# Borders by token block, five weight slots and turned-back first chunks in a four-layer transformer kernel

## The reference

```python
for i in range(2):                       # first block
    y = mla_mixer(...) if i == 0 else dilated_mixer(...)   # on rms_norm(h, g[0])
    h = h + rms_norm(y, g[1])
    h = h + rms_norm(swiglu(rms_norm(h, g[2]), w_in, w_out), g[3])
    h = h + (p[i] @ ple_w_proj[i]) * sigmoid(h @ ple_w_gate[i])
for l in range(2):                       # second block
    mix = hybrid_mixer(x, w_in[l], ...)  # retention, block attention, convolution; then @ w_out
    x = layer_norm(ALPHA * x + mix, ...)
    f = (gelu(causal_dwconv(x @ w_up_a)) * (x @ w_up_b)) @ w_down
    x = layer_norm(ALPHA * x + f, ...)
```

## Time and profile before

| | us |
|---|---|
| median of 3 runs | 1621.08 (1620.62 to 1624.9) |
| the profiled execution | 1619.89 |
| its span in the trace | 1618.1 |
| PE busy | 1494.7 (92%) |
| POOL busy | 1060.0 (66%) |
| DVE busy | 840.3 (52%) |
| ACT busy | 756.2 (47%) |

### The profile page before, as it was taken

One profiled execution on the slowest core, in us unless ns is written; L12 is line 12 of the kernel. 1 busy time (PEld: TensorE's weight loads), 2 busy tenths in 40 slices (PEclk: granted clock), 3 DMA queues, 4 the chain that ended last, 5 costly groups with the idle time before them and its releaser, 6 DMA issues.

```text
span 1618.1 us, 26225 instructions
## 1 busy us (share of the span) xinstructions
PE 1494.7 (92%) x10190; PEld 1372.1 (85%) x10190; DVE 840.3 (52%) x1269; ACT 756.2 (47%) x856; POOL 1060.0 (66%) x255
## 2 busy tenths in 40 slices
PE   6897999998999999989999999779999797799996
PEld 5786999878999999789987789679998697599985
DVE  5546888024222322388841254567860458568833
ACT  6774554344544444555543445235543344255531
POOL 4254788865665555568887586358888575378883
PEclk9997999999999999989999999879999899799999
DMA  5383555545555555345555555335565555245551
GB/s 208 98 293 123 182 181 182 182 156 180 174 184 162 167 171 172 130 144 181 181 182 182 183 189 182 104 105 182 181 208 182 168 172 175 78 148 183 182 214 53
DMA packets 63346, 271.15 MB, mean 168 GB/s; under 512 B 5978, under 2 KB 28688, under 8 KB 36273
## 3 DMA queue, kind: packets, MB, share of 16 engines
q1 hardware_dynamic: 38300, 242.62, 44.3%
q10 hardware_dynamic: 24981, 27.61, 5.1%
HBM read 269.08 MB, written 8.21 MB: 171 GB/s over the span
## 4 chain that ended last, share of the span: by engine, by line
PE 83%; DVE 11%; ACT 4%; issue 1%; POOL 1%; DMA 0%; ACTq 0%; SPq 0%; DVEq 0%
PE psum L423 81%; DVE rstd L1337 2%; DVE newton L1331 1%; PE psum L740 1%; PE psum L530 1%; ACT w_hi L917 1%; ACT xt_hi L932 1%; DVE psum L1480 1%; DVE cv L1692 1%; DVE psum L1470 1%; POOL w_lo L403 1%; DVE h L1484 1%; DVE cv L1688 0%; DVE var L1716 0%; DVE xt_lo L1410 0%
## 5 line engine op out<-in xcount | busy, mean ns | idle before, releaser
L403 POOL TENSOR_TENSOR w_lo<-raw,w_hi 128x2048 fp32r<-128x2048 f32 (+3 forms) x251 | 1059.8, 4228 | 535.5 <-ACT w_hi L917 535.2
L917 ACT ACTIVATE w_hi<-raw 128x2048 fp32r<-128x2048 f32 (+3 forms) x251 | 450.2, 1794 | 515.9 <-PE psum L423 497.0
L423 PE MATMUL psum<-xt_hi,w_hi 128*128 128x256 f32 x1984 | 569.6, 287 | 7.1 <-DVE xt_lo L1410 5.8
L423 PE MATMUL psum<-xt_hi,w_lo 128*128 128x256 f32 x1984 | 565.9, 285 | 0.0
L423 PE MATMUL psum<-xt_lo,w_hi 128*128 128x256 f32 x1984 | 565.9, 285 | 0.0
L423 PEld LDWEIGHTS psum<-xt_hi,w_hi 128*128 128x128 f32 x1984 | 385.7, 194 | 14.8 <-issue 14.7
L423 PEld LDWEIGHTS psum<-xt_lo,w_hi 128*128 128x128 f32 x1984 | 385.7, 194 | 0.1
L423 PEld LDWEIGHTS psum<-xt_hi,w_lo 128*128 128x128 f32 x1984 | 385.3, 194 | 0.0
L423 PE MATMUL psum<-w_hi,xt_hi 128*128 128x384 f32 (+3 forms) x408 | 143.3, 364 | 15.7 <-DVE xt_lo L1414 9.5
L1443 DVE TENSOR_TENSOR conv<-conv,gate 128x256 f32<-128x256 f32 x44 | 144.8, 3292 | 1.5
L423 PE MATMUL psum<-w_hi,xt_lo 128*128 128x384 f32 (+3 forms) x408 | 140.2, 357 | 0.0
(11 more groups left out here) (214 smaller groups left out, 1484.5 us busy)
## 6 DMA issues: line engine op xcount, KB each, us to landing
raw<-w_tail SPq DMA_DIRECT2D x156, 1024.0 KB, 4.9
raw<-w_dil SPq DMA_DIRECT2D x24, 1024.0 KB, 4.8
raw<-w_mix SPq DMA_DIRECT2D x24, 1024.0 KB, 4.8
raw<-w_dil SPq DMA_DIRECT2D x16, 576.0 KB, 4.0
bias_tiles<-bias_rows ACTq DMA_DIRECT2D x1, 6912.0 KB
gbuf<-gain_rows ACTq DMA_DIRECT2D x12, 512.0 KB, 5.4
dbias<-bias_tiles ACTq DMA_DIRECT2D x16, 384.0 KB, 4.9
raw<-w_mla_a SPq DMA_DIRECT2D x3, 1024.0 KB, 7.9
```

The lines of the kernel that those rows point to most:

```text
L403: nc.gpsimd.tensor_tensor(w_lo[:, s, 0:width], raw[:, s, 0:width], w_hi[:, s, 0:width].bitcast(F32), ALU.subtract).then_inc(lo_split, 1)
L423: return nc.tensor.matmul(dst, lhsT, rhs, start=start, stop=stop)
L917: nc.scalar.activation(w_hi[:, s, 0:width], raw[:, s, 0:width], ACT.Copy).then_inc(hi_split, 1)
```

## The change

- **Five slots, the low half in place.** SLOTS is 5. `w_lo` takes the memory of `raw`: POOL writes its difference over the chunk it reads. SP therefore waits until chunk c-5 is used; ACT's split no longer waits for a use. The split of an MLA chunk has the chunk's own width (before: 2048 columns for two in three). `ahead(c, lead)` splits all chunks up to c+lead, and lead is 3 (LEAD) in FFN, output and PLE stages.
- **Stages end by token block.** `wide_end` holds the last three chunks (HOLD): block 0 of all three, then block 1. The next stage's block 0 is turned (`turn_block(then, 0)`) before block 1 of the last chunk, or halfway in it (layers 2 and 3). At wo0 and wo1 the held blocks stand between the attention's last steps.
- **Stages begin by token block.** `begin` computes block 0 of its chunks, turns block 1, computes block 1. In the PLE, block 0 of the gate and of the projection come before block 1 of the gate.
- **First chunks turned back.** `begin_tiles` gives an FFN's first 2 (layers 0, 1) or 3 chunks, and the dilated stage's first 2, with the tokens stationary, block by block; ACT copies the results to SBUF (`copy_rows`), PE transposes them into the banks where `tiles_product` would have put them, four transposes a chunk.
- **ACT and DVE order.** `border` has ACT do, for each block: squares of y, the turned copies, squares of h; ahead of block 1's copies it splits the next chunk. DVE writes `xt_lo` of a block right after its `h`. In the FFN ACT's activation stands before the split.
- `p_hi` and `p_lo` are made in each layer in `ot_hi`, `ot_lo`; `gate`, `conv` and `cv` share memory. SP, POOL, PE and ACT have no loops any more.

```diff
-SLOTS = 3
+SLOTS = 5
+GROUP = 6
+LEAD = 3
+HOLD = 3
+LANES = 3
...
+ROWS_AT = {T_FFN0: ((3, 4), (7, 0)), T_DIL: ((4, 5), (6, 7)), T_FFN1: ((0, 1), (3, 4)),
+           T_FFN2: ((0, 1, 6), (7, 0, 1)), T_FFN3: ((0, 1, 6), (7, 0, 1))}
...
-        raw = sb("raw", [P, SLOTS, W])
+        with ExitStack() as part:
+            raw = sb("raw", [P, SLOTS, W], F32, part)
+        w_lo = sb("w_lo", [P, SLOTS, W], F32R)
         w_hi = sb("w_hi", [P, SLOTS, W], F32R)
-        w_lo = sb("w_lo", [P, SLOTS, W], F32R)
...
-                    sp.wait_ge(lo_split, c - SLOTS + 1 + per * i)
+                    sp.wait_ge(chunk_used, c - SLOTS + 1)
...
+            def begin(t, cs, cols, part):
+                views = []
+                for k, c in enumerate(cs):
+                    views.append(chunk(c, cols))
+                    part(k, *views[k], 0)
+                turn_block(t, 1)
+                for k, view in enumerate(views):
+                    part(k, *view, 1).then_inc(chunk_used, 1)
+
+            def begin_tiles(t, c, bank0):
+                held = len(ROWS_AT[t][0])
+                def part(k, hi, lo, tb):
+                    tok = slice(tb * P, (tb + 1) * P)
+                    if tb == 1:
+                        pe.wait_ge(rows_copied, ROWS_BEFORE[t] + held)
+                    for kt in range(KT):
+                        arrive(t, tb, kt)
+                        ins = split_x(psum[:, ROWS_AT[t][tb][k], 0:2 * P], xt_hi[:, kt, tok], xt_lo[:, kt, tok],
+                                      hi[:, kt, :], lo[:, kt, :], kt == 0, kt == KT - 1)
+                    ins.then_inc(rows_made, 1)
...
+                for k in range(held):
+                    part(k, *views[k], 1)
+                for k in range(held):
+                    pe.wait_ge(rows_copied, ROWS_BEFORE[t] + held + k + 1)
+                    for half in range(2):
+                        for tb in range(TB):
+                            at = half * SEQ + tb * P
+                            ins = nc.tensor.transpose(psum[:, bank0 + k, at:at + P],
+                                                      first_rows[:, k, tb, half * P:(half + 1) * P], ident[:, :])
+                    ins.then_inc(chunk_used, 1)
+                return held
...
+            def wide_end(c, n, lhs, at, then, late, down=False, ready=lambda k: None):
+                first = n - HOLD
+                views = []
+                for k in range(HOLD):
+                    views.append(chunk(c + first + k, D))
+                    ready(k)
+                    ins = wide_block(0, first + k, *views[k], n, lhs, at, down)
                 ins.then_inc(y0_ready, 1)
...
+                    if k == HOLD - 1 and then is not None:
+                        turn_early = lambda: turn_block(then, 0)
+                        if not late:
+                            turn_early()
+                        ins = wide_block(1, first + k, *view, n, lhs, at, down, turn_early if late else None)
...
+                held = begin_tiles(t, C_IN[l], FFN_AT[l])
                 if l < 2:
                     turn_r((2, 4)[l], t)
...
+                for u in range(held, FT):
+                    if u >= LANES:
+                        pe.wait_ge(hidden_ready, l * FT + u - LANES + 1)
+                    tiles_product(C_IN[l] + u, FFN_AT[l] + u % LANES)
...
+            pe.wait_ge(d_ready, 6)
+            wo2 = wo_part(1, 2)
+            wo2(0)
             d_turn(last, 1)
+            wo1(1).then_inc(chunk_used, 1)
             d_values_sum(last, 1)
-            wo_end(1, lambda k: pe.wait_ge(d_ready, 6 + 2 * k))
+            pe.wait_ge(d_ready, PAIRS)
+            wo3 = wo_part(1, 3)
+            wo3(0).then_inc(y0_ready, 1)
+            wo2(1).then_inc(chunk_used, 1)
+            wo3(1).then_inc(chunk_used, 1)
+            turn_block(T_FFN1, 0)
...
+            def ahead(c, lead=2):
+                while split[0] < min(c + lead + 1, CHUNKS):
+                    hi_part(split[0])
+                    split[0] += 1
...
+            def border(t, y, c, normed):
                 for tb in range(TB):
+                    if y is not None:
+                        y_squares(y, tb)
+                    if tb == 1:
+                        ahead(c, LEAD)
+                        copy_rows(t, 0)
                     turn_hi_block(t, xt_hi, tb)
+                    if normed:
+                        act.wait_ge(rows_ready, rows_of(t) + tb + 1)
+                        h_squares(tb)
+                copy_rows(t, 1)
...
+                ahead(C_IN[l], LEAD)
+                for u in range(FT):
+                    act.wait_ge(conv_ready, l * FT + u + 1)
+                    nc.scalar.activation(gate[:, u % LANES, :], conv[:, u % LANES, :], func).then_inc(gate_ready, 1)
+                    ahead(C_IN[l] + u + 1, LEAD)
...
-                turn_lo_rest(t)
+                    turn_lo_block(t, xt_hi, xt_lo, tb)
```

More of the change, by code:

```diff
@@ L376, in _ @@
             sp.dma_start(table[0:BUCKETS, NG * 16:], rel_table_2).then_inc(bias_src_in, 16)
-            at = C_MLA
+            c = C_MLA
             for name, n, widths in STAGES[1:]:
[L380 to L388, removed]
+                for i in range(n):
+                    for u in range(len(widths)):
+                        stream(name, i, u, c)
+                        c += 1
             for tb in range(TB):
@@ new lines, in begin_tiles @@
+            def begin_tiles(t, c, bank0):
+                held = len(ROWS_AT[t][0])
+                made = [0]
+                def part(k, hi, lo, tb):
[9 more added lines that the diff above has]
+                for k in range(held):
+                    views.append(chunk(c + k, 2 * P))
+                    part(k, *views[k], 0)
+                turn_block(t, 1)
+                for k in range(held):
+                    part(k, *views[k], 1)
+                for k in range(held):
+                    pe.wait_ge(rows_copied, ROWS_BEFORE[t] + held + k + 1)
[6 more added lines that the diff above has]
+                return held
@@ L476, in tiles_product @@
+            def tiles_product(c, bank):
+                hi, lo = chunk(c, 2 * P)
                 for half in range(2):
@@ L531, in turn_block @@
                     ins.then_inc(turned, 1)
-            def turn(t, src, ready):
-                for tb in range(TB):
-                    turn_block(t, src, ready, tb)
-            def block_ready(t):
-                return lambda tb: pe.wait_ge(rows_ready, rows_of(t) + tb + 1)
             def turn_r(count, t):
@@ L694, in _ @@
             last = MLA_STEPS - 1
             mla_scores(last)
-            for m in range(2):
-                pe.wait_ge(ot_ready, m + 1)
-                wo(0, m)
+            pe.wait_ge(ot_ready, 1)
+            wo(0, 0)
+            pe.wait_ge(ot_ready, 2)
+            wo1 = wo_part(0, 1)
+            wo1(0)
             mla_probs(last)
-            pe.wait_ge(ot_ready, last)
-            wo(0, 2)
+            pe.wait_ge(ot_ready, 3)
+            wo2 = wo_part(0, 2)
+            wo2(0)
             mla_sum(last, lambda: None)
+            wo1(1).then_inc(chunk_used, 1)
@@ L895, in _ @@
                 t = (T_RET2, T_RET3)[n]
-                turn(t, t1, block_ready(t))
+                for tb in range(TB):
+                    turn_block(t, tb, t1)
                 pe.wait_ge(cv_copied, 3 * n + 3)
@@ L967, in load_gain, with copy_rows @@
+            def copy_rows(t, tb):
+                if t in ROWS_AT:
+                    held = len(ROWS_AT[t][0])
+                    for k in range(held):
+                        act.wait_ge(rows_made, ROWS_BEFORE[t] + tb * held + k + 1)
+                        nc.scalar.activation(first_rows[:, k, tb, :], psum[:, ROWS_AT[t][tb][k], 0:2 * P],
+                                             ACT.Copy).then_inc(rows_copied, 1)
             def load_gain(row, slot):
@@ L1070, in mla_heads @@
                     after()
-                ahead(c + 1, more, turns)
+                ahead(c + 1)
             def mla_qT(step):
@@ L1121, in _ @@
             act.dma_start(bias_tiles, toeplitz).then_inc(tiles_stored, 16)
[L1122 to L1127 removed]
+            for step in range(1, MLA_STEPS - 1):
+                mla_heads(step + 1, lambda: mla_exp(step))
+                mla_pT(step)
+                mla_qT(step + 1)
+                ahead(C_MLA + 3 * step + 5)
+                mla_out(step)
             last = MLA_STEPS - 1
@@ L1286, in _ @@
                                      ACT.Copy).then_inc(m_hi, 1)
-                turn_hi((T_RET2, T_RET3)[n], ot_hi)
-                for m in range(1, PROJ_N):
-                    ahead(C_WO[l] + m)
-                turn_hi(T_FFN[l], xt_hi)
+                for tb in range(TB):
+                    turn_hi_block((T_RET2, T_RET3)[n], ot_hi, tb)
+                for m in range(1, PROJ_N - 1):
+                    ahead(C_WO[l] + m, LEAD)
+                border(T_FFN[l], None, C_WO[l] + PROJ_N - 1, False)
                 ffn(l)
```

(1 more changed line is left out.)

522 lines of the change are left out of this document (229 added, 293 removed).

## The result

The changed kernel takes 1685.57 us (median of 4 runs, 1684.08 to 1687.13) against 1620.85 for the kernel before (4 runs, 1619.95 to 1624.9): a ratio of 1.0394, 95% interval 1.0374 to 1.0415. It is 65 us slower; the forecast was 1615.5 and the range ended at 1628.

The account below looks back on a forecast made before the run. PE, busy 1494.7 us or 92% of the span, was taken as the bound. Border, tail and MLA terms summed to 5.5 us gained: 1619.9 to 1614.4 for the profiled execution, median 1615.5, range 1593 to 1628.

Parts of the forecast that it names:

- Five slots, low half in place: Chunk loading and POOL's subtraction throughout: loads arrive in time and POOL keeps its 4.5 us, so effect 0.
- A: Border wo0 to ffn0: idle and clock loss 14.2 us against 15.3, including 4.4 waiting for block 1's h; gain 1.1.
- D: Border wo1 to ffn1: 18.2 us idle and clock, two waits opened by halved cover (1.4 scores-to-exponentials, 1.85 last output); loss 5.4.
- E: Border wo2 to ffn2, again at wo3: 12.65 us left, with new 6.35 stall before fourth chunk; gain 3.7 each.
- margin of 0.17 us: At four borders, POOL's subtraction starts 0.17 us before DVE's second-block h, which then comes 4.4 us later.
- rival 1: At four borders DVE gets block 1's h in before POOL, so it is not blocked: 23 us, 1592; chance 0.2.
- B and B2: Borders out0 to ple0 and out1 to ple1: 8.0 each, 3.8 for blocked h, 1.55 after turn; losses 5.3 and 4.4.
- C: Border ple0 to dil: 5.3 us left, including gap 2.05, turning back 1.1 and 1.3 for tile 2; gain 1.0.
- G: Border out2 to mix3: 6.9 us left, waits of 0.4+0.25, 2.8 and 1.05 plus clock 2.4; gain 5.5.
- F: Border ple1 to mix2: waits of 1.05 and 0.3 us left; gain 1.5.
- rival 2: POOL's subtraction catches the layer norm's first-block h at E (twice) and G: 16 us slower, 1631; chance 0.15.
- MLA term: Attention chunks split at their own width, ahead of ACT's probability copy: 0.7 us saved in each of three; gain 2.2.

Follow-up runs that it names:

- e5_border: The change with the dropped wait back in the FFN loops, and block 1's next split issued behind ACT's last work at the four norm borders: 1623.41 us.
- e7_paced_plain: The change with the dropped wait back, and FFNs turning both blocks at once with the plain tile product for all chunks: 1624.03 us.
- e6_early: The change with the dropped wait back, and each FFN's fourth chunk split before ACT copies block 1's rows: 1658.7 us.
- e8_both: The change with the dropped wait back and the edits of both e5_border and e6_early: 1616.24 us.
- e14_start: Like e8_both, but two PLE borders as in the change, and FFN2's and FFN3's sixth-chunk split held until the fourth is used: 1621.99 us.
- e9_gate: The change plus a POOL wait: an FFN input chunk's subtraction starts only once DVE has finished the tile four back; no wait on ACT: 1636.89 us.

## Why the prediction was wrong

**The step that failed** is "*Five slots, low half in place* ... Nothing". It asked whether loads, slots and POOL's own time would suffice; they do. It did not ask what else the dropped wait held apart. e1_paced, which puts this wait back in the FFN loops alone, is 48.6 us faster. ACT's wait for chunk c-3 was not needed for the five slots, but it spaced the subtractions at PE's 5.76 us, and in the 1.13 between them DVE had the rest of its tile. "PE never waits inside an FFN" was read as room; it was the result of that spacing. The prediction had named "gaps inside a stage" as what would show it wrong.

**The same omission stands in two terms of the sum.** The stall before the fourth chunk was put at 1.5 (A, D) and 6.35 (E, twice), 15.7 in all, with one subtraction over the hidden rows. It was 30.9. At E two stood there:
```profile
1119.02 2.40 DVE L1496 CAST ht_hi<-lanes 128x256 f32 x1
1121.54 4.51 DVE L1497 TENSOR_TENSOR ht_lo<-lanes,ht_hi 128x256 f32 x1
```
```profile
1116.76 9.01 POOL L408 TENSOR_TENSOR w_lo<-raw,w_hi 128x2048 fp32r<-128x2048 f32 x2 [16.31 <-ACT w_hi L962]
```
The clock is the third: its terms came to 4.4 less than before, and it was 12.8 more. Inner waits 39.3, start 15.2 and clock 17.2 make 71.7; the profiled execution took 1686.3 against the 1614.4 forecast for it, 71.9 more. The agreement is closer than the account: PE's busy time in two chunks with pairs is 11.77 (23.54 in the first window, halved) where 11.52 is enough without, some 7 us over the stages (an estimate), which this sum leaves out, and smaller errors of both signs at the borders offset it.

**What held.** The margin of 0.17 us at the four borders fell as forecast, at A so:
```profile
141.17 4.61 POOL L408 TENSOR_TENSOR w_lo<-raw,w_hi 128x2048 fp32r<-128x2048 f32 x1 [9.71 <-ACT w_hi L962]
```
```profile
141.37 5.50 DVE L1448 SCALAR_TENSOR_TENSOR h<-t,rstd,h 128x1024 f32<-128x1024 f32 x1
```
Four of the eight `h` took 5.5, so rival 1 did not come. B and B2: 3.56 and 1.50 (forecast 3.8 and 1.55). C: 2.05 and 1.24 (2.05 and 1.3). D's opened waits: 1.19 and 1.87 (1.4 and 1.85). G: 0.36, 2.77 and 0.98 (0.65, 2.8, 1.05). F: 0.98 (1.05). E: 0.59 and 1.07 (0.6 and 1.05), with h0 unblocked, so rival 2 did not come either. At A and D PE stood 2.4 for `h1` and not 4.4; around A it had come later, at a granted clock of 0.83 from 137 to 147. In e1_paced, which has the same program there and a clock of 1.00, it stood 3.81, so what this term lost the clock's gained. The MLA term was 1.5 (3.4 to 1.9) and not 2.2. Some workings do not come out as written: for E's fourth chunk 0.5, 1.92, 4.6, 0.3 and 0.43 make 7.75 and not 8.0; of A's 1.5 before the fourth chunk the working shows 0.3 (7.4 against 7.1) and no size for the wait on the hidden rows; 1.92 by proportion of 1152 to 2048 columns is 1.08 and not 1.2. None of them matters beside the step that failed. By the borders alone the change would have been about even. That is argued and no run shows it: e5_border (1623.4) and e7_paced_plain (1624.0), which have no pairs, have other borders too.

**Still open.** What decides between the two steady states is shown only by cases: late and early splits moved it, but no run changed the phase of one tile alone, and e6_early, e8_both and e14_start (one of twelve at 1634.7) have executions that stand apart from the rest. Nor was it tried what the missing table loads do.

## To carry to other kernels

A wait that the data no longer needs may still keep two engines out of each other's way. Before it is dropped, look at what runs in the gaps it makes, on every engine that can be blocked by the one it paces. Where an engine locks another out for a whole instruction, price two such instructions in a row against one tile, not one: in a closed loop the delay can release the next pair. And try the bar on the engine that blocks: on a shared queue it holds up what is behind it (e14_start). That bar has a price as well, where it lengthens a tile beyond PE's time and where it ends (e9_gate).

## What the runs showed of the hardware

- A DVE cast of 128x256 with one operand in SBUF is held by POOL's subtraction (0.29 alone, 2.54 here), as is an operation with two (0.43, 4.59). Operations on DVE that read PSUM keep their 0.42 to 0.48 while POOL runs. POOL's time hardly grew by it: 4.63 alone, 9.22 for two in FFN2 and 9.38 in FFN0. The Trainium skill ("SBUF — State Buffer", Who interferes with whom) says that the one that issues first has the shared ports for its whole instruction and that casts can be among the blocked; the rows agree.
- An FFN of the same program can run in either of two steady states: 5.76 us a chunk, or 12.8 to 13.5 for two. In the change it repeats (its four runs lie within 0.2%), in e6_early one run of four is 11 us away from the rest.
- With waits of 1.0 and 1.7 us inside a stage the granted clock stayed at 1.00 (first window above, and 1.00 from 222 to 248 in FFN0), but for one stretch of 3.4 us at half clock from 1234.2, behind the wait that ended at 1233.99. In the stalls of 5 and 10 us before the fourth chunks it fell to half each time.
